# A 128-wide projection for the second mixer's output gate, computed as seven products of half blocks instead of eight

## The reference, cut to what matters

```
z = jnp.matmul(h, w_in)
aq, ak, av, ag, alr, bq, bk, bv, bg, bbeta, bdec, mg = split_cols(z)
qkv = silu(conv_grid(concatenate([bq, bk, bv]), gdn_conv))     # 1536 channels, 3x3 taps on an 8x64 grid
bq = l2norm(qkv[queries]) * GDN_DK ** -0.5
bk = l2norm(qkv[keys])
...
yb = rmsnorm(ob, gdn_onorm) * silu(bg)                          # bg: 512 tokens x 512 channels
```

## Time and profile before

| | |
|---|---|
| runs | 1341.34 us median of 3 (1338.7 to 1341.41) |
| profiled execution | 1342.3 us; span 1340.5 us |
| granted TensorE clock, mean | 0.995 of 2.4 GHz |
| busy share of the span | TensorE 96%, VectorE 52%, ScalarE 31%, GpSimd 30% |
| the chain that ended last | TensorE 89% |
| the stage "conv", TensorE | up to about 340.8 us after the span's start |

### The profile page before, as it was taken

One profiled execution on the slowest core, in us unless ns is written; L12 is line 12 of the kernel. 1 busy time (PEld: TensorE's weight loads), 2 busy tenths in 40 slices (PEclk: granted clock), 3 DMA queues, 4 the chain that ended last, 5 costly groups with the idle time before them and its releaser, 6 DMA issues.

```text
span 1340.5 us, 23888 instructions
## 1 busy us (share of the span) xinstructions
PE 1291.7 (96%) x9603; PEld 795.4 (59%) x9603; DVE 694.0 (52%) x1422; ACT 413.0 (31%) x897; POOL 396.9 (30%) x470
## 2 busy tenths in 40 slices
PE   5999999999999999999999999998999999998997
PEld 3554655555666777778445786445655786445653
DVE  4366657846333434464465374237736383337735
ACT  4244303362432222201014102236623202236721
POOL 0100000211324443154530250127731150127731
PEclk9999899999999999999999999999999999999999
DMA  9710112101310100031254415110002515100001
GB/s 315 269 63 27 39 64 78 62 1 64 119 73 3 65 2 3 3 126 64 87 192 95 133 32 188 64 52 1 2 16 67 153 41 188 63 1 2 1 1 63
DMA packets 71533, 96.54 MB, mean 72 GB/s; under 512 B 27640, under 2 KB 35248, under 8 KB 71423
## 3 DMA queue, kind: packets, MB, share of 16 engines
q1 hardware_dynamic: 71050, 94.76, 21.1%
q10 hardware_dynamic: 372, 0.27, 0.1%
HBM read 92.89 MB, written 2.13 MB: 71 GB/s over the span
## 4 chain that ended last, share of the span: by engine, by line
PE 89%; DVE 4%; POOL 2%; ACT 2%; issue 1%; DMA 1%; ACTq 0%; SPq 0%; POOLq 0%; DVEq 0%
PE PS L147 85%; PE PS L2785 2%; DVE AR L2891 1%; ACT AR L3013 1%; POOL AR L3072 1%; DMA AR<-in_onehot 1%; DMA AR<-in_final_g 1%; POOL AR L2008 1%; PE PS L353 0%; POOL AR L3070 0%; DVE AR L2878 0%; ACT AR L3023 0%; PE PS L2119 0%; DVE AR L2061 0%; PE PS L1395 0%
## 5 line engine op out<-in xcount | busy, mean ns | idle before, releaser
L147 PE MATMUL PS<-AR 64*64 64x64 f32 (+14 forms) x8966 | 1218.8, 332 | 22.4 <-ACT AR L3023 6.5
L147 PEld LDWEIGHTS PS<-AR 128*128 128x128 f32 (+4 forms) x8966 | 725.4, 155 | 488.2 <-issue 392.0
L3013 ACT ACTIVATE AR<-AR 128x257 f32<-128x257 f32 (+5 forms) x160 | 84.9, 531 | 98.4 <-DVE AR L2891 89.0
L2891 DVE CUSTOM_DVE_ANT_0 AR<-PS,AR 128x257 f32<-128x257 f32 (+5 forms) x160 | 72.3, 452 | 60.7 <-PE PS L147 43.1
L412 POOL TENSOR_TENSOR AR<-AR 128x1 f32<-128x1 f32 (+4 forms) x26 | 21.9, 843 | 260.4 <-DVE AR L407 213.7
L1183 DVE SCALAR_TENSOR_TENSOR AR<-AR 128x441 f32<-128x441 f32 (+2 forms) x96 | 78.6, 819 | 15.7 <-ACT AR L1140 12.0
L1570 DVE TENSOR_TENSOR AR<-PS,AR 128x256 f32<-128x256 f32 x60 | 25.5, 425 | 100.7 <-PE PS L147 97.6
L3072 POOL TENSOR_SCALAR AR<-AR 128x257 f32<-128x257 f32 (+5 forms) x96 | 53.8, 560 | 58.5 <-DVE AR L2897 51.0
L3070 POOL TENSOR_SCALAR AR<-AR 128x128 f32<-128x128 f32 (+3 forms) x64 | 39.2, 613 | 63.1 <-DVE AR L2897 58.2
L1697 ACT ACTIVATE AR<-PS 128x512 f32<-128x512 f32 x48 | 28.7, 597 | 92.5 <-PE PS L147 90.1
L2008 POOL TENSOR_TENSOR AR<-AR 128x512 f32<-128x512 f32 x36 | 47.7, 1326 | 28.2 <-DMA AR<-in_w_o 25.2
(11 more groups left out here) (264 smaller groups left out, 941.8 us busy)
## 6 DMA issues: line engine op xcount, KB each, us to landing
AR<-in_w_in SPq DMA_DIRECT2D x16, 2048.0 KB, 8.9
AR<-in_w_mod SPq DMA_DIRECT2D x6, 2048.0 KB, 12.7
AR<-in_w_out SPq DMA_DIRECT2D x4, 2048.0 KB, 12.6
AR<-in_x SPq DMA_DIRECT2D x8, 512.0 KB, 5.6
AR<-in_w_in SPq DMA_DIRECT2D x4, 1024.0 KB, 7.4
AR<-in_w_o SPq DMA_DIRECT2D x2, 2048.0 KB, 7.8
AR<-in_w_in SPq DMA_DIRECT2D x2, 1664.0 KB, 8.7
AR<-in_w_in SPq DMA_DIRECT2D x12, 256.0 KB, 4.2
```

Source lines behind the costliest of these rows:

```text
L147: return t.matmul(o, l, r, start=s, stop=p, skip_group_check=True)
L2891: v.do.tensor_tensor_reduce(PB[j % NJP][e][:, 0:nk], ps["s", l, j, e][:, 0:nk], bias_for(qb, kind, 2 * a + e, nk), 1.0, 3e38, ALU.add, ALU ...
L3013: a_.do.activation(P, P, ACT.Exp, bias=mn[:, j % NJS, e:e + 1], scale=-1.0, accum_out=su[:, j % NJS, e:e + 1]).then_inc(sa, na("p", l, j, e))
```

## The change

The gate is made in pairs of channel tiles (p = 0, 1). The features are cut in two halves, the two tiles of a pair give two halves of the channels, the tokens two halves; each pair becomes seven products of [128 channels x 512 features] by [512 features x 256 tokens], four matmuls each, instead of eight. What the seven products need: sums and differences of the weights (four per pair, by GpSimd, behind the squares of m = 7 and ahead of L1207), differences of the tokens (four, by VectorE, between the taps of m = 7 and of m = 8), a copy of the first product out of PSUM (ScalarE), seven additions per pair (VectorE, behind all taps). Silu is then applied from SBUF to SBUF. `delta_t` no longer waits for the end of VectorE's stage but for its taps and the token differences. The four banks of tiles become eight banks of pairs, and the ring leaves gam's bank out from there on.

```diff
+    T1b, T2b, T3b, T4b = (AR[:, BT_at + 1024 * i:BT_at + 1024 * i + 1024].rearrange("p (k n) -> p k n", k=4) for i in range(4))
+    be_, bf_, bg_, bh_ = (hT[:, 4 * (i // 2):4 * (i // 2) + 4, 256 * (i % 2):256 * (i % 2) + 256] for i in range(4))
+    SHARED = ((1, 2), (6, 7), (5, 3), (4,))
+    def sums_of_rows_b(v):
+        for i, o, x, y in ((1, T1b, bf_, be_), (2, T2b, bh_, T1b), (3, T3b, bh_, bf_), (4, T4b, bg_, T2b)):
+            v.do.tensor_tensor(o, x, y, ALU.subtract).then_inc(sv, nv("bT", i))
+    def sums_of_weights_b(g, p):
+        w, = weights(g, 7)
+        a, b, c, d = bg_blocks(w, p)
+        s1, s2, s4_ = SB[p]
+        for i, o, x, y, op in ((1, s1, c, d, ALU.add), (2, s2, s1, a, ALU.subtract), (3, c, a, c, ALU.subtract), (4, s4_, b, s2, ALU.subtract)):
+            g.do.tensor_tensor(o, x, y, op).then_inc(sg, ng("bS", p, i))
+    def seven_bg_t(t, p, w):
...
+        for k in range(4):
+            o = ps.take(t, "b7", p, k)
+            for i, what in enumerate(SHARED[k]):
...
+                for q in range(4):
+                    x = mm(t.go, o[:, 256 * i:256 * i + 256], left[:, q, :], right[:, q, :], q == 0, q == 3)
+            x.then_inc(st, nt("b7", p, k))
+    def seven_bg_v(v, p):
...
+        v.wait_ge(sa, na["g1b", p])
+        sum_of(A[:, 0:256], 0, 1, g1)
+        ps.empty(sv, nv, "b7", p, 0)
+        sum_of(u2, 1, 0, g1)
+        sum_of(u3, 1, 1, u2)
+        ps.empty(sv, nv, "b7", p, 1)
+        sum_of(B[:, 256:512], 2, 0, u3)
+        sum_of(u2, 2, 0, u2)
+        sum_of(A[:, 256:512], 2, 1, u2, "bg", 2 * p)
+        ps.empty(sv, nv, "b7", p, 2)
+        sum_of(B[:, 0:256], 3, 0, u3, "bg", 2 * p + 1)
+        ps.empty(sv, nv, "b7", p, 3)
@@ conv_t
-        for h in range(4):
-            if h % 2 == 0:
-                decay_sums(t, h // 2)
-            p = ps.take(t, "bg", h)
-            projT(t, p, w, 128 * h, 128, 256, 768, ("bg", h))
+        for p in range(2):
+            decay_sums(t, p)
+            ps.ring = [b for b in range(8) if b != ps.of["gam",]]
+            seven_bg_t(t, p, w)
@@ conv_a
+        for p in range(2):
+            a.wait_ge(st, nt["b7", p, 0])
+            a.do.activation(G1b[p], ps["b7", p, 0][:, 0:256], ACT.Copy, bias=0.0, scale=1.0).then_inc(sa, na("g1b", p))
         for h in range(4):
-            a.wait_ge(st, nt["bg", h])
-            a.do.activation(gateB[h], ps["bg", h][:, :], ACT.Silu, bias=0.0, scale=1.0).then_inc(sa, na("bg", h))
-            ps.empty(sa, na, "bg", h)
+            a.wait_ge(sv, nv["bg", h])
+            a.do.activation(gateB[h], gateB[h], ACT.Silu, bias=0.0, scale=1.0).then_inc(sa, na("bg", h))
@@ conv_v
+            if m == 7:
+                sums_of_rows_b(v)
+        nv.mark("inputs", "delta")
+        for p in range(2):
+            seven_bg_v(v, p)
@@ conv_g
+        for p in range(2):
+            sums_of_weights_b(g, p)
@@ delta_t
-        t.wait_ge(sv, nv["at", "conv"])
+        t.wait_ge(sv, nv["inputs", "delta"])
```

More of the change, by code:

```diff
@@ L1076, in program @@
     sqs = [Cv(64 * x_.shape[1]) for x_, _ in segs]
+    BT_at = Cv.b
+    T1b, T2b, T3b, T4b = (AR[:, BT_at + 1024 * i:BT_at + 1024 * i + 1024].rearrange("p (k n) -> p k n", k=4) for i in range(4))
+    SB = [[AR[:, BT_at + 4096 + 512 * (3 * p + i):BT_at + 4608 + 512 * (3 * p + i)].rearrange("p (k n) -> p k n", k=4) for i in range(3)]
+          for p in range(2)]
+    assert BT_at + 7168 <= TOT - 2048
+    oBf = oB.rearrange("p a n -> p (a n)")
+    G1b, GUb = ([oBf[:, 512 * k + 256 * i:512 * k + 256 * i + 256] for i in range(2)] for k in range(2))
@@ new lines, in program, with bg_blocks @@
+    gateB = [AR[:, TOT - 2048 + 512 * h:TOT - 1536 + 512 * h] for h in range(4)]
+    be_, bf_, bg_, bh_ = (hT[:, 4 * (i // 2):4 * (i // 2) + 4, 256 * (i % 2):256 * (i % 2) + 256] for i in range(4))
+    SHARED = ((1, 2), (6, 7), (5, 3), (4,))
+    NEED_S, NEED_T = {5: 1, 6: 2, 7: 3, 3: 4}, {5: 1, 6: 2, 7: 3, 4: 4}
+    def bg_blocks(w, p):
+        return [w[:, 4 * (i % 2):4 * (i % 2) + 4, 256 * p + 128 * (i // 2):256 * p + 128 * (i // 2) + 128] for i in range(4)]
+    def sums_of_rows_b(v):
+        for i, o, x, y in ((1, T1b, bf_, be_), (2, T2b, bh_, T1b), (3, T3b, bh_, bf_), (4, T4b, bg_, T2b)):
+            v.do.tensor_tensor(o, x, y, ALU.subtract).then_inc(sv, nv("bT", i))
@@ new lines, in sums_of_weights_b @@
+    def sums_of_weights_b(g, p):
[5 more added lines that the diff above has]
+    def seven_bg_t(t, p, w):
+        a, b, c, d = bg_blocks(w, p)
+        s1, s2, s4_ = SB[p]
+        for k in range(4):
+            o = ps.take(t, "b7", p, k)
+            for i, what in enumerate(SHARED[k]):
+                if what in NEED_S:
+                    t.wait_ge(sg, ng["bS", p, NEED_S[what]])
+                if what in NEED_T:
+                    t.wait_ge(sv, nv["bT", NEED_T[what]])
+                left, right = {1: (a, be_), 2: (b, bg_), 3: (s4_, bh_), 4: (d, T4b), 5: (s1, T1b), 6: (s2, T2b), 7: (c, T3b)}[what]
+                for q in range(4):
+                    x = mm(t.go, o[:, 256 * i:256 * i + 256], left[:, q, :], right[:, q, :], q == 0, q == 3)
+            x.then_inc(st, nt("b7", p, k))
@@ new lines, in seven_bg_v, with sum_of @@
+    def seven_bg_v(v, p):
+        def sum_of(o, k, i, x, *name):
+            v.wait_ge(st, nt["b7", p, k])
+            v.do.tensor_tensor(o, ps["b7", p, k][:, 256 * i:256 * i + 256], x, ALU.add).then_inc(sv, nv(*name))
+        A, B = gateB[2 * p], gateB[2 * p + 1]
+        g1, (u2, u3) = G1b[p], GUb
+        v.wait_ge(sa, na["g1b", p])
[10 more added lines that the diff above has]
+        ps.empty(sv, nv, "b7", p, 3)
@@ L1227, in program @@
     assert mark2[0] + 5120 + 2048 <= gap_hi
-    gateB = [AR[:, TOT - 2048 + 512 * h:TOT - 1536 + 512 * h] for h in range(4)]
     merged = AR[:, TOT - 8192:TOT - 4096].rearrange("p (m n) -> p m n", m=8)
```

## The result

The changed kernel takes 1347.86 us, median of 4 runs (1345.96 to 1348.54), against 1341.2 us (1338.7 to 1341.41, 4 runs): a ratio of 1.0053, 95% interval 1.0041 to 1.0066, that is 7.1 us slower (5.5 to 8.9). I forecast 1345.1 us, 3.8 us slower.

The account below looks back on a forecast made before the run. TensorE, busy 96% of the span, was taken to set the pace. Products -3.30, l2 wait +5.2, stage end +0.55 and pg's bank +1.33 summed to +3.8 us: 1345.1 us on the median, range 1340.3 to 1348.3.

Parts of the forecast that it names:

- the clock's term: TensorE's clock behind the new pauses: taken to stay at full rate, so no time was added for it.
- the sum: All terms over the kernel added up: -3.30 + 5.2 + 0.55 + 1.33 = +3.8 us.
- TensorE's products: In "conv": 27.52 us of gate products replaced by two pairs of seven at 24.22 us, a gain of 3.30 us.
- GpSimd's sums on VectorE's time: Beside the taps of m = 8: eight sums slow VectorE by 0.9 us each, 7.2 us (3.5 to 10.2).
- VectorE's own: Ahead of the taps of m = 8: four token differences make them 2.48 us late, hidden if alone.
- What waits behind these taps: In the l2 products: late Silu and Ln free bank 1 late; TensorE stands still 5.0 us, loss 5.2 us.
- The end of the stage: End of "conv": an addition ahead of the last Silu makes VectorE and ScalarE 0.55 us later (0.3 to 0.8).
- The bank under pg: Start of "delta": pg's banks now hold kN 1 and vN 1, freed two reads later, 1.33 us (0 to 1.4).
- The rival on the clock: Clock falls in the new l2 pause, losing 1.7 us: +5.5 us in all, 1346.8 us; chance 0.19.

Follow-up runs that it names:

- experiment 1: Changed kernel with GpSimd's eight sums of weights held until VectorE's taps of m = 8 are done; ratio 0.9998 to the kernel before.
- experiment 7: Changed kernel with VectorE's four token differences behind the taps of m = 8, GpSimd's sums still beside the taps; ratio 1.0017 to the kernel before.
- experiment 3: Changed kernel with only the ring moved on by three places ahead of delta; ratio 1.0048 to the kernel before.
- experiment 4: Kernel before with only the ring moved on by four places ahead of delta; ratio 1.0012 to the unedited kernel before.
- experiment 9: Changed kernel with both pauses filled: product l2 7 eleven times more, transposes of vN 1 six times more; median 1343.78 us, ratio 1.0031.
- experiment 10: Changed kernel run again unaltered on the same chip; median 1347.63 us, ratio 1.0057 to the kernel before.
- experiment 8: Changed kernel, sums of weights and token differences behind the taps of m = 8, ring moved three places, vN 1 transposes twice more; 1338.74 us.
- experiment 2: Changed kernel with GpSimd's sums behind the taps of m = 8 and the ring moved on three places ahead of delta; ratio 0.9988 to the kernel before.
- experiment 6: Changed kernel with product l2 7 repeated eleven times and the transposes of vN 1 three times more; ratio 1.0052 to the kernel before.
- experiment 5: Changed kernel with product l2 7 repeated eleven times in the pause ahead of l2 8; ratio 1.0055 to the kernel before.

## Why the prediction was right in its way and wrong in its size

The direction and the places were right. The size was not: 3.8 us forecast, 7.1 measured. The median, 1347.86 us, is 0.4 us inside the top of the range; as a difference, 7.1 us is just over its 7.0 (1348.3 - 1341.34).

The step that failed is the clock's term, which the sum put at nothing. It measured 1.1 + 2.4 = 3.5 us; every other term came within 0.3 us.

- *TensorE's products.* -3.30 us forecast, -3.3 measured.
- *GpSimd's sums on VectorE's time.* 7.2 us forecast, 6.8 measured as 9.3 less the 2.5 of VectorE's own: 0.85 us for each sum. The sum's own length alone is 10.35 / 8 = 1.29 us (experiment 1). The Trainium skill (SBUF — State Buffer, SBUF: two separate sides) has the other engine blocked for all of it; the taps lost two thirds. The rule names the right pair and says rightly that they exclude each other; its price is too high for these operations.
- *What waits behind these taps.* 5.0 us of standing still forecast, 4.7 seen. I had said that the differences alone would be hidden, which is so (experiment 1), and counted the two delays as a plain sum, which is not: the sums alone leave a wait of 0.4 us, where the plain sum gives 2.4 (experiment 7).
- *The end of the stage.* 0.55 forecast, 0.8 measured. 0.4 us of it pass between the end of the last Silu and L1605, where the profile names no wait; before it was less than 0.1. Why, is open.
- *The bank under pg.* 1.33 forecast, 1.4 measured, shown alone by experiments 3 and 4.
- *The rival on the clock.* I held a fall of the clock to be the less likely case, at 0.19 against 0.42, on the strength of one pause of 1.3 us that had left the clock alone, and I priced it for one pause only. There were two pauses, of 4.7 and 3.5 us, and the clock fell in both, in both profiles of the changed kernel. It cost 3.5 us in the first profile, and about as much in the timed runs by experiments 9 and 10. Worse, I had misread the trace: "this trace has one fall" is wrong. It has a second, at 147 us, behind a gap of 1.29 us (the rows are in the section on the result), as long as the pause that I called as evidence against a fall. Read in full, the trace had lost the clock around pauses of 1.1 us and 1.3 us and kept it behind one of 1.3, so pauses of 5 and 3 us, as I forecast them, should have had a price in the sum. The rule of the Trainium skill (TensorE: Matmul & The Clock Gate, Part 1: The HAM clock gate), by which idleness brings back the half rate, agrees with every trace here that has a pause of 2.7 us or more. I had quoted it and then weighed it below a single row.
- *The sum against the profiled span.* The two spans differ by 3.7 us, which fits the sum of 3.8 by accident; the early stages had run 3.85 us faster in the execution after.

## What to carry to other kernels

When an engine that never waits is about to be made to wait, price the pause and then the clock behind it: here two pauses made 8.2 us of standing still where there had been 1.3, and with them 3.5 us lost to the half rate. Read the whole trace of the kernel before for falls, not only the neighbourhood of the change. Work given to GpSimd "for free" is paid by VectorE if VectorE is busy beside it (here 0.85 us of the taps, which read two operands from SBUF, for each sum of 1.29); place it where VectorE rests, and ask who waits for VectorE. A changed count of ring buffers changes which buffer a later stage meets: look up what the fixed takes behind it will find.

## What the runs showed of the hardware that I had not expected

- The granted clock can fall around pauses as short as 1.0 to 1.3 us (at 145 to 147 us, five of twelve profiles, 3.0 us lost in the kernel before), and need not: behind other pauses of 0.9 to 1.3 us, ahead of pg, it stayed at full (the kernel before, experiments 8 and 9). Pauses of 2.2 us lost it twice (experiments 2 and 3) and once not (experiment 6); all of 2.7 us and more did.
- The fall can come after work has begun again: 0.4 us behind the end of the pause ahead of pg in experiment 10, 0.6 in experiments 5 and 7, 1.0 in experiment 3, 1.5 in experiment 2.
- Two things that slow an engine need not add: 2.5 us of own work and 5.0 us of contention gave 9.3 us (experiment 7 against the changed kernel).
- Redundant products can pay: with 4.7 us and 3.1 us of repeated work the changed kernel is 3.5 us faster than without (experiments 9 and 10).
